# Norm tails with per-tile sums and unread products, and GpSimd low parts with PSUM accumulators, in a two-layer SSD/conformer block

## The reference

```
y   = (silu(u @ wg) * (u @ wu)) @ wd            # d_ff = 2816, u = rmsnorm(h) * g * (1+scale) + shift
h   = h + weight * gate * rmsnorm(y, g_post)    # the tail: post norm, gate, residual
u   = modulate(h) @ w_in                        # 5152 columns: SSD x/B/C, dt, z, conformer, short conv
y   = [rmsnorm(ssd(silu(dwconv5(xBC))) * silu(z)), silu(layernorm(dwconv31(v*sigmoid(g)))), b * dwconv3(c*h)]
h   = h + gate * rmsnorm(y @ w_out, g_post)
```

## Time and profile before

| | |
|---|---|
| time, median of 3 runs | 2434.33 us (2433.19 to 2437.06) |
| the profiled execution's own time | 2439.39 us |
| its span, first to last instruction | 2437.7 us |
| PE busy | 2207.7 us, 91% |
| DVE, ACT, POOL busy | 1304.1, 1019.9, 73.7 us |
| mean granted TensorE clock | 0.939 |

### The profile page before, as it was taken

How to read it: one execution, slowest core, us unless ns; L and a number is a source line. 1 busy time by engine, 2 the same in 40 slices (tenths; PEclk the granted TensorE clock), 3 DMA queues, 4 the chain that set the end, 5 groups by cost and what they waited for, 6 DMA issues and landing times. The chain is left out here.

```text
span 2437.7 us, 27823 instructions
## 1 busy us (share of the span) xinstructions
PE 2207.7 (91%) x11297; PEld 1850.0 (76%) x11297; DVE 1304.1 (53%) x1795; ACT 1019.9 (42%) x1525; POOL 73.7 (3%) x74
## 2 busy tenths in 40 slices
PE   5999999978888989799999988999996888888998
PEld 5788888856676767588888776888885676777997
DVE  4544454257969843544444345333325688855554
ACT  5543443244364343444343334232324444555443
POOL 0000000010101000100000000000001001000000
PEclk8899999979999989799999998999996998988999
DMA  6455545212233212245545441332321233333553
GB/s 214 140 172 162 167 152 168 95 38 68 88 102 96 79 53 87 80 155 162 171 158 167 148 134 56 101 103 87 130 95 54 70 105 95 105 115 119 182 181 122
DMA packets 282542, 291.00 MB, mean 119 GB/s; under 512 B 8286, under 2 KB 275502, under 8 KB 282414
## 3 DMA queue, kind: packets, MB, share of 16 engines
q1 hardware_dynamic: 281619, 287.04, 36.5%
q10 hardware_dynamic: 795, 2.18, 0.3%
HBM read 288.02 MB, written 1.18 MB: 119 GB/s over the span
## 5 line engine op out<-in xcount | busy, mean ns | idle before, releaser
L93 DVE TENSOR_TENSOR split<-raw,split 128x1024 fp32r<-128x1024 f32 (+1 forms) x368 | 442.9, 1203 | 749.9 <-ACT split L85 749.9
L85 ACT ACTIVATE split<-raw 128x1024 fp32r<-128x1024 f32 (+1 forms) x368 | 382.7, 1040 | 915.3 <-PE bank L126 906.4
L124 PE MATMUL bank<-uh,split 128*128 128x512 f32 (+1 forms) x1344 | 489.0, 364 | 1.1 <-DVE split L93 1.1
L125 PE MATMUL bank<-ul,split 128*128 128x512 f32 (+1 forms) x1344 | 489.0, 364 | 0.0
L126 PE MATMUL bank<-uh,split 128*128 128x512 f32 (+1 forms) x1344 | 489.0, 364 | 0.0
L126 PEld LDWEIGHTS bank<-uh,split 128*128 128x128 f32 x1344 | 254.3, 189 | 40.5
L124 PEld LDWEIGHTS bank<-uh,split 128*128 128x128 f32 x1344 | 254.5, 189 | 38.7 <-issue 1.5
L125 PEld LDWEIGHTS bank<-ul,split 128*128 128x128 f32 x1344 | 254.3, 189 | 36.7
L124 PE MATMUL bank<-mix_uh,split 128*128 128x512 f32 (+1 forms) x608 | 237.9, 391 | 38.7 <-DVE split L93 22.1
L124 PE MATMUL bank<-hh,split 128*128 128x512 f32 (+1 forms) x704 | 257.0, 365 | 0.9 <-DVE split L93 0.9
L126 PE MATMUL bank<-hh,split 128*128 128x512 f32 (+1 forms) x704 | 255.9, 364 | 0.0
(11 more groups left out here) (224 smaller groups left out, 2653.2 us busy)
## 6 DMA issues: line engine op xcount, KB each, us to landing
raw_mod<-in_w_mod SPq DMA_DIRECT2D x64, 1024.0 KB, 4.8
raw<-in_ffn_w_gate SPq DMA_DIRECT2D x44, 1024.0 KB, 5.1
raw<-in_ffn_w_up SPq DMA_DIRECT2D x44, 1024.0 KB, 5.1
raw<-in_w_in SPq DMA_DIRECT2D x40, 1024.0 KB, 5.1
raw<-in_ffn_w_down SPq DMA_DIRECT2D x32, 1024.0 KB, 4.9
raw<-in_w_out SPq DMA_DIRECT2D x16, 1024.0 KB, 4.9
raw<-in_ffn_w_down SPq DMA_DIRECT2D x16, 768.0 KB, 4.2
decay<-cum_rows SPq DMA_DIRECT2D x48, 256.0 KB, 3.6
```

The lines of the kernel that those rows point to most:

```text
L85: ins = K.nc.scalar.activation(K.wh[:, half, 0:kn, :], K.raw[:, slot, 0:kn, half * P:half * P + P], ACT.Copy)
L93: ins = K.nc.vector.tensor_tensor(K.wl[:, half, 0:kn, :], K.raw[:, slot, 0:kn, half * P:half * P + P], r32(K.wh[:, half, 0:kn, :]), ALU.su ...
L124: K.nc.tensor.matmul(bank[:, 0:tn], K.wh[:, half, k, :], h, start=first and k == 0, stop=False)
L125: K.nc.tensor.matmul(bank[:, 0:tn], K.wh[:, half, k, :], l, start=False, stop=False)
```

## The change

Four things are changed.

1. In every norm, ACT now takes the root straight from the sums in PSUM (scale and epsilon inside the instruction), DVE takes the reciprocal, and PE broadcasts with one 128x128 matmul for each 128 tokens, whose weights are the factor's column repeated. The scaling instruction and the diagonal are gone.
2. In the tails, the second norm's sums are made for each of 8 tiles instead of 4 pairs, in the order in which tiles come; GpSimd adds tiles 0, 1, 3, 4 and 6, and DVE tiles 2, 5 and 7, whose product it keeps in a PSUM bank. DVE's two low parts for the next block (`split_ahead_dve`) stand behind the second reciprocal instead of ahead of it, and the gain of the next norm is made earlier in the output product (`pre_gain_dve`).
3. PE gets matmuls that nobody reads (`warm_pe`, 128x256, into bank 4): 3 ahead of the first sums, 2 behind them, 6 behind the broadcast, 2 behind the second sums, and 8 at the start of each block's first pair.
4. In `mix_in`, GpSimd makes most low parts (34 of 38 in layer 0, 30 of 38 in layer 1), the conformer taps accumulate in banks 2 and 3 and the SSD convolution in banks 6 and 7, and the state products move to banks 4 and 5.

```diff
+def weight_lo_pool(K, pool, slot, half, kn, nth):
+    pool.wait_ge(K.hi_done.sem, K.hi_done.at(nth + 1))
+    ins = K.nc.gpsimd.tensor_tensor(K.wl[:, half, 0:kn, :], K.raw[:, slot, 0:kn, half * P:half * P + P],
+                                    r32(K.wh[:, half, 0:kn, :]), ALU.subtract)
+    ins.then_inc(K.lo_pool.inc(), 1)
...
-    pe.wait_ge(K.lo_done.sem, K.lo_done.at(nth + 1))
+    pe.wait_ge(*(low or (K.lo_done.sem, K.lo_done.at(nth + 1))))
...
     behind = 3
+    warm_pe(K, 8)
     pe.wait_ge(K.lo_done.sem, K.lo_done.at(2))
...
+def rstd_act(K, act, tok, width, stats, nth):
     n = tok[1] // P
+    act.wait_ge(K.stat_done.sem, K.stat_done.at(stats))
+    ins = K.nc.scalar.activation(K.ms[:, 0:n], K.bank[5][:, 0:n], ACT.Sqrt, scale=1.0 / width, bias=K.eps[:, 0:1])
+    ins.then_inc(K.ms_ready.inc(), 1)
+def rstd_dve(K, dve, tok, nth):
     n = tok[1] // P
+    dve.wait_ge(K.ms_ready.sem, K.ms_ready.at(nth))
...
+    K.nc.vector.reciprocal(K.rstd[:, 0:n], K.ms[:, 0:n]).then_inc(K.rstd_ready.inc(), 1)
 def rstd_pe(K, pe, tok, nth):
+    pe.wait_ge(K.rstd_ready.sem, K.rstd_ready.at(nth))
+    for t in range(tok[1] // P):
+        ins = K.nc.tensor.matmul(K.bank[6][:, t * P:t * P + P], K.rstd[:, t:t + 1].to_broadcast([P, P]), K.ident[:, :],
+                                 start=True, stop=True)
     ins.then_inc(K.rb_ready.inc(), 1)
...
-POOL_TILES = 5
+POOL_TILES = (0, 1, 3, 4, 6)
+OWN_TILES = (2, 5, 7)
+SQUARE_ORDER = (0, 2, 1, 3, 5, 4, 6, 7)
+def residual_dve(K, dve, tok, y, nth):
+    rstd_dve(K, dve, tok, nth)
     dve.wait_ge(K.y_ready.sem, K.y_ready.at(8))
     dve.wait_ge(K.rb_ready.sem, K.rb_ready.at(nth))
+    own = 0
+    for j in range(8):
+        if j in POOL_TILES:
+            K.nc.vector.tensor_tensor(y[:, j, 0:tn], y[:, j, 0:tn], K.bank[6][:, 0:tn], ALU.mult).then_inc(K.yr_ready.inc(), 1)
+            continue
+        part = K.bank[own][:, 0:tn]
+        own += 1
+        K.nc.vector.tensor_tensor(part, y[:, j, 0:tn], K.bank[6][:, 0:tn], ALU.mult).then_inc(K.yb_ready.inc(), 1)
+        dve.wait_ge(K.yb_ready.sem, K.yb_ready.at(own))
+        ins = K.nc.vector.tensor_tensor(K.res[:, j, t0:t0 + tn], K.res[:, j, t0:t0 + tn], part, ALU.add)
+        ins.then_inc(K.res_tail.inc(), 1)
...
 def residual_rms_pe(K, pe, tok, y, nth, norms_before):
-    pair_sums_pe(K, pe, y, tok, norms_before)
+    warm_pe(K, 6)
+    for n, j in enumerate(SQUARE_ORDER):
+        pe.wait_ge(K.square_ready.sem, K.square_ready.at(8 * norms_before + n + 1))
+        sums_pe(K, pe, y[:, j, :], tok, n == 0, n == 7)
+    warm_pe(K, 2)
     rstd_pe(K, pe, tok, nth)
+def warm_pe(K, n):
+    for _ in range(n):
+        K.nc.tensor.matmul(K.bank[4][:, 0:2 * P], K.ident[:, :], K.tri[:, :, :].rearrange("p d n -> p (d n)"), start=True, stop=True)
...
+        warm_pe(K, 3)
         pe.wait_ge(K.sq_added.sem, K.sq_added.at(7))
         sums_pe(K, pe, K.sq[:, 0, :], self.tok, True, True)
+        warm_pe(K, 2)
         rstd_pe(K, pe, self.tok, self.norms)
...
+        self.lo_on_dve = tuple(range(SCAN_AT + 1, SCAN_AT + 9)) if last else (SCAN_AT + 1, SCAN_AT + 2, SCAN_AT + 8, SCAN_AT + 9)
...
+            for n in range(2, SCAN_AT + 1):
+                if n not in plan.lo_on_dve:
+                    weight_lo_pool(K, pool, n // 2 % 2, n % 2, 8, n)
...
-                    nc.scalar.activation(M.xbc[:, tile, :], acc[:, tile % 2, :], ACT.Silu).then_inc(K.xbc_out.inc(), 1)
+                    nc.scalar.activation(M.xbc[:, tile, :], K.bank[6 + tile % 2][:, :], ACT.Silu).then_inc(K.xbc_out.inc(), 1)
...
-                            ins = nc.vector.scalar_tensor_tensor(out, src(k), weights(k), out, ALU.mult, ALU.add)
+                            ins = nc.vector.scalar_tensor_tensor(out if signal else total, src(k), weights(k), total, ALU.mult, ALU.add)
...
-                if 2 <= n < NH:
+                if n in plan.lo_on_dve:
                     weight_lo(K, dve, n // 2 % 2, n % 2, 8, n)
```

More of the change, by code:

```diff
@@ L112, in split_ahead_dve, with product_half @@
         ins.then_inc(K.lo_done.inc(), 1)
-def product_half(K, pe, bank, half, kn, xh, xl, tok, first, last, nth, ready=None, after_k=None):
+def product_half(K, pe, bank, half, kn, xh, xl, tok, first, last, nth, ready=None, after_k=None, low=None):
     t0, tn = tok
-    pe.wait_ge(K.lo_done.sem, K.lo_done.at(nth + 1))
+    pe.wait_ge(*(low or (K.lo_done.sem, K.lo_done.at(nth + 1))))
     for k in range(kn):
@@ L316, in prenorm_act, with pre_gain_dve @@
         K.nc.scalar.activation(uh[:, j, t0:t0 + tn], un[:, 0:tn], ACT.Copy).then_inc(K.uh_ready.inc(), 1)
+def pre_gain_dve(K, dve, layer, which):
+    nc = K.nc
+    scale = K.mod[:, layer, 8 * (3 * which + 1):8 * (3 * which + 2), :]
+    dve.wait_ge(K.mod_evac.sem, K.mod_evac.own())
+    nc.vector.tensor_scalar(K.gain[:, :, :], scale, 1.0, None, ALU.add).then_inc(K.dve_step.inc(), 1)
+    dve.wait_ge(K.dve_step.sem, K.dve_step.own())
+    g = K.par[:, layer, 0, 72 + 8 * which:80 + 8 * which].unsqueeze(2).to_broadcast([P, 8, 2])
+    nc.vector.tensor_tensor(K.gain[:, :, :], K.gain[:, :, :], g, ALU.mult).then_inc(K.dve_step.inc(), 1)
 def prenorm_dve(K, dve, layer, which, tok, un_buf, uh, ul):
@@ L442, in residual_rms_pe, with __init__ @@
+    warm_pe(K, 2)
     rstd_pe(K, pe, tok, nth)
+def warm_pe(K, n):
+    for _ in range(n):
+        K.nc.tensor.matmul(K.bank[4][:, 0:2 * P], K.ident[:, :], K.tri[:, :, :].rearrange("p d n -> p (d n)"), start=True, stop=True)
 class OutProduct:
-    def __init__(self, K, w, parts, order, xh, xl, tok, xtok, y, halves, panels, stats, norms, norm_follows, gain, mods=0,
+    def __init__(self, K, w, parts, order, xh, xl, tok, xtok, y, halves, panels, stats, norms, next_norm, gain, mods=0,
                  mod_h=0, mod_layer=0, mod_q=0):
@@ L551, in dve @@
                 self.gain(dve)
+            if n == 2 and self.next_norm:
+                pre_gain_dve(K, dve, *self.next_norm)
             if self.mods and n == self.mods + 1:
@@ L927, in _ @@
                     states += 1
+            for n in range(plan.lo_on_dve[-1] + 1, NH):
+                weight_lo_pool(K, pool, n // 2 % 2, n % 2, 8, n)
         @block.tensor
@@ L1139, in _ @@
                         act.wait_ge(K.xbc_out.sem, K.xbc_out.own())
-                        nc.scalar.activation(acc[:, tile % 2, :], bank[:, :], ACT.Identity, scale=par[:, 2, 24 + tile:25 + tile],
+                        nc.scalar.activation(K.bank[6 + tile % 2][:, :], bank[:, :], ACT.Identity, scale=par[:, 2, 24 + tile:25 + tile],
                                              bias=par[:, 2, 60 + tile:61 + tile])
@@ L1177, in _ @@
                         pass
-            rstd_act(K, act, part, 1)
+            rstd_act(K, act, part, GRP_T * P, GRP_T, 1)
             split_ahead_act(K, act)
@@ L1799, in closing @@
     K.end_phase()
-FILLER = 80
+FILLER = 64
 def hybrid_block(nc, inputs, out):
@@ L1954, in hybrid_block @@
             feed_forward(K, layer, 2, LATENT if last else FULL, None if last else layer + 1, 0, not last,
-                         0 if last else 24, after)
+                         0 if last else 24, after, None if last else (layer + 1, 0))
         closing(K)
```

136 lines of the change are left out of this document (52 added, 84 removed).

## The result

The changed kernel takes 2393.94 us (median of 4 runs, 2391.97 to 2397.97). The kernel before took 2435.69 on the same chip (4 runs, 2433.19 to 2439.6). The ratio is 0.9829, with a 95% interval from 0.9809 to 0.985. That is 41.7 us less; the forecast was 31.3 less, 2403 us, with the range 2376 to 2430. The profiled execution spans 2396.2 us, before it was 2437.7.

The account below looks back on a forecast made before the run. PE is busy 91% of the span, so a change pays only where PE waits or runs at half clock. 6.5 + 1 + 0 + 2.8 + 15 + 5 + 1 = 31.3 off 2434.3 gives 2403 us, range 2376 to 2430.

Parts of the forecast that it names:

- first norm of six tails: First norm of each tail: unread matmuls hold the clock, 1.1 us gained each, 6.5 us (bounds -3.6 and +11.4).
- second norm of five tails: Second norm of tails: sums gain nothing at falling clock, gain instructions leave the block's start; +1 us (bounds -7, +27).
- 8 unread at block starts: Unread matmuls at each block's start: win nothing, since DVE paces the first pair; 0, bound -6 in all.
- four mixer norms: The four norms inside the mixers lose the diagonal and the scaling: +2.8 us (0 to 4).
- turns 8 to 12: In `mix_in`: GpSimd's low part 9 is there earlier, 8.6 us in layer 0, 6.4 in layer 1; +15 (0 to 22).
- scan: `mix_in`, n = 18 to 31: DVE relieved of low parts, less GpSimd's stops; net +5 us (-20 to +20), -5 by the skill's rule.
- z and 256-token halves, rest of `mix_in`: `mix_in`: 4 us of DVE work saved in layer 0, -0.6 for each of five 256-token halves; +1 us (-8 to +10).
- price for GpSimd's low parts stopping DVE: In the scan, each of GpSimd's nine low parts stops DVE once: 10 to 13 us given back.
- the pitch of about 3.4: 256-token halves in layer 1: high part, GpSimd's low part and handovers make a 3.4 us pitch instead of 2.8.
- The clock did not hold through the sums: Rival: the clock holds through the second norms' sums, 5.5 us more in each of five tails; 2377 us, chance 0.13.
- DVE's freed time: Rival: in `mix_in` DVE's freed time is off the path, so 15 + 5 are lost; 2423 us, chance 0.17.
- GpSimd stops DVE for more than it frees: Rival: DVE waits through 64 GpSimd low parts, losing 81 us, half where DVE bounds: +40; 2463 us, chance 0.12.

Follow-up runs that it names:

- mix_only: The kernel before with the whole of the new `mix_in` (GpSimd's low parts, accumulators and state products in banks); old norms, no unread matmuls: 2415.73 us, 0.9919.
- tails_only: The changed kernel with `mix_in` as before (low parts on DVE, accumulators in SBUF), only state products staying in banks 4 and 5: 2417.43 us, 0.9932.
- no_unread: The changed kernel without any of its unread matmuls (236 instructions fewer): 2406.88 us, 0.9879.
- cols128: The changed kernel with each sum matmul moving the whole 128x128 matrix of ones instead of one column: 2380.78 us, 0.9768.
- no_start8: The changed kernel without only the 8 unread matmuls at each block's start: 2398.84 us, 0.9836.
- acc_sbuf: The changed kernel with both convolution accumulators back in SBUF, GpSimd still making its low parts: 2446.87 us, 1.0055.
- the square above: Four kernels, GpSimd's low parts or not by accumulators in SBUF or banks: the low parts cost 30 us with SBUF, gain 21 with banks.
- cols_no_unread: The changed kernel with 128-column sums and DVE's two low parts ahead of the second reciprocal, without any unread matmul: 2382.74 us, 0.9773.
- wide_sums: The changed kernel with second-norm sums as one matmul a tile against a ones matrix, root and reciprocal of the whole bank: 2384.84 us, 0.9788.

## Why the forecast came out right, step by step

The direction and the range were right. The size was short by 10 of 41.7 us, and the steps missed by up to 8 us, some one way and some the other, so that the total lies as near as it does is partly luck. The forecast for `mix_in` (15 + 5 + 1 = 21) met `mix_only` (19.7); that for the norms (6.5 + 1 + 2.8 = 10.3) fell short of `tails_only` (16.6).

The steps below are sized from the two profiled executions, by the times between the last product, the first multiplication and the next `un`, and by the table of halves.

| step of the forecast | forecast | measured |
|---|---|---|
| first norm of six tails | 6.5 | 5.4 |
| second norm of five tails | 1 | 9.3 |
| 8 unread at block starts | 0 | 0 |
| four mixer norms | 2.8 | 1.1 |
| turns 8 to 12 | 15 | 10.5 |
| scan | 5 | 10.5 |
| z and 256-token halves, rest of `mix_in` | 1 | -0.9 |
| sum | 31.3 | 35.9 |

The measured sum meets the two parts run alone (36.3). The remaining 5.5 of the 41.5 between the profiles lie in the opening and in the products of the feed-forwards, which the change does not touch; in the second of them, the one behind the first mixer, these products took, from the end of the first pair, 426.4 us before, 424.0 after, 424.4 in `tails_only` and 421.8 in `no_unread`. What sets them in one kernel or another was not tried and stays open.

- **First norm.** The number came out near, but the mechanism held in one tail only. The forecast gave the gain to the held clock. In the first tail 1.9 us were gained as forecast, about half of it by the clock (`no_unread` kept 1.0 of it). In the next three the broadcast of `no_unread` took 1.16, 1.44 and 1.16 us, where the kernel before took 1.47, 2.07 and 2.07: with the shorter chain the clock held for all or most of it without unread matmuls. In the two of 256 tokens it took 0.6 to 0.7 us in all three. In the third the unread ones stood in the way: the sums ended 4.7 us behind the last product of the feed-forward for 3.4. The step is worth 5.4 us with them and 6.0 without: luck, as to its cause.
- **Second norm: the term that was mis-sized, 1 us for 9.3.** It took the clock to fall "from the third tile on" or "in between" and so the sums to gain nothing. Here the unread matmuls did their work: without them these norms are 3.3 us longer than in the kernel before. The clock fell 7 us after the first multiplication of the first tail; the sums gained 4.5 us over five tails (12.7, 12.4, 13.7, 14.3 and 6.0 for four times 14.0 and 7.7), the handovers and broadcast behind them 1.3 where a loss was forecast (the 256-token tail alone fell from 3.2 to 1.4, for there the clock held to the end), and the gain instructions 3.5 for the 4.3 forecast. That sums do not hold the clock was right in the four full-width tails; `cols128` shows that it is their one column.
- **Block starts.** Right, and `no_start8` shows it.
- **Turns 8 to 12.** PE's wait for half 9 is gone, as forecast. High part 12 follows high part 9 by 27.8 us where it was 31.8: 4 us sooner for the 7 forecast; half 12 ends 31.9 us behind half 8 for 28.7. Two things were left out: DVE's dt product stopped for 2.2 us by GpSimd's low part 10, on ACT's path to high part 11; and half 10, at half clock behind PE's wait, took 7.5 us from its first matmul to its last (6.9 in the kernel before) where the forecast gave it 6.2. Layer 1 gained 5.2 for the 6.4 forecast.
- **Scan.** Twice the forecast, 10.5 for 5. The forecast let 12 low parts leave DVE in layer 0 and about 5 in layer 1; it is 10 and 6, which leaves its 20 us of relief as they were. Its price for GpSimd's low parts stopping DVE was 10 to 13 us. In the whole trace 7 of 48 decays were stopped, for 10.2 us together, so the price was about right; how much of it was on the path, and why the gain is larger than the difference, was not taken apart. One of them, beside its GpSimd low part:

```profile
659.03 2.35 POOL L100 TENSOR_TENSOR split<-raw,split 128x1024 fp32r<-128x1024 f32 x1 [6.89 <-ACT split L85]
659.55 2.37 DVE L1278 TENSOR_TENSOR decay<-decay,cb 128x512 f32<-128x512 f32 x1
```

- **z and 256-token halves.** The signs were right (+3.0 in layer 0's z, -3.6 in layer 1); the pitch of about 3.4 was too low, 4.0 where a GpSimd low part was late.
- **Rivals.** The clock did not hold through the sums of the four full-width tails. DVE's freed time was on the path (`mix_only`, 19.7 us). That GpSimd stops DVE for more than it frees is what happens with the accumulators in SBUF: for the rival's 81 us of lost DVE time (64 low parts at 1.26 us) `acc_sbuf` shows 80, though from 46 stops, and for its +40 us in the time the square above shows +30. The banks are what decided.
- **The Trainium skill** was cited for DVE and GpSimd ("SBUF — State Buffer", who interferes with whom). The traces agree in both directions: GpSimd first, and a decay ends with it (above); DVE first, and GpSimd's low part takes 2.91 us for 2.35 in the scan. What the forecast made of it for the scan, -5, was not met: it took DVE to be stopped for up to 2.5 us by each of nine low parts; seven decays were stopped, for 1.5 us each.
- **And for the clock**, the Trainium skill's "TensorE: Matmul & The Clock Gate" (Part 1, "HAM oscillation") puts a lost clock down to gaps in which PE idles. The first broadcast of the kernel before agrees (PE busy 0.96 of 2 us at 490 to 492, clock 0.55), and so does half 10 (PE idle 4.8 us, then 0.50). The second sums do not: PE was busy 2.00 of 2.00 us while the clock fell, and after it, so here the measurement decides.

## What to carry to other kernels

Work given to GpSimd beside a busy DVE paid here when DVE's accumulators lay in PSUM, so that its taps had one SBUF input (21 us gained, where with the accumulators in SBUF 30 were lost); judge the two edits as one. Where a chain of tiny matmuls bounds a stretch, first widen what they move, before adding matmuls that nobody reads: filler helps in a gap and costs where PE is full. And a step that ends at the same time in every kernel (18.5 us here) says that nothing put ahead of it counts.

## What the hardware showed that was not expected

- Eight sum instructions with 128 columns took 1.16 us at full clock (`cols128`) against 1.05 with one column (the changed kernel), beside 0.97 us of weight loads in both: the columns are nearly free.
- The granted clock came back from 0.50 to 1.00 while such sums ran (494 to 500 in `cols_no_unread`), and never did with one-column sums, full as PE was (496 to 508 in `no_unread`).
- DVE's reciprocal costs 3.37 us for 128x512 in a bank (`wide_sums`), 0.95 for 128x128 and 0.18 for 128x4, where multiplications and additions take 0.69 for 128x512.
- DVE writes and reads a bank as accumulator at the speed of SBUF (taps 747 ns in the changed kernel, 761 before).
- GpSimd's subtraction of 128x1024 takes 2.41 us, DVE's 1.24.
